# The expert gates G in HBM: by quarter of a tile, or by partition and block of eight expert tiles

## Chip, cores and metric

One Trainium2 chip, one core. The metric is the time of one execution on the device in microseconds; the kernel before takes 4118.97 us (median of 3 runs, 4109.92 to 4119.53).

## The reference

One step of a decoder layer: an input projection feeds a 4-head mLSTM and 8-head stick-breaking attention, their output is projected, gated and added, and then comes PEER, the part that matters here. Tokens: 1024 of a prompt and 64 of a sample, D = 1024.

```python
qry = (xf @ w_query).reshape(T, 8, 2, 128)
sa = einsum('thd,nd->thn', qry[:, :, 0], sub_keys_a)      # 128 scores
sb = einsum('thd,nd->thn', qry[:, :, 1], sub_keys_b)
va, ia = top_k(sa, 16); vb, ib = top_k(sb, 16)
top_s, pos = top_k(all 256 sums va + vb, 16)
experts = take(ia * 128 + ib, pos)                        # 16 per head, of 16384
gates = softmax(top_s)
act = gelu(einsum('tkd,td->tk', expert_u[experts], xf))
out = einsum('tk,tkd->td', gates * act, expert_v[experts])
```

## The kernel before

The phases follow one another: projection, gates, prompt_mix, sample_mlstm, sample_attention, and then the two that the change touches, `routing` (L1789) and `apply` (L2164), the expert stage.

**Two ways to the experts.** Of the nine token tiles of 128 rows, four (D0 to D1, 512 tokens, TD) are dense: for them all 16384 experts are computed and multiplied by a matrix of gates G that is zero but for the chosen ones. The other five (640 rows, the sample as a half tile of 64 picks) gather: for each of 576 picks, POOL fetches a row of expert_u and a row of expert_v per partition by indirect DMA.

**G** has one value for each expert (a, b), 128 by 128, and each dense token. The expert is numbered 128 a + b; b lies on the partitions. `routing` makes it: for each dense tile DVE builds one-hot matrices (`hot`, L2113), ACT scales one by the gates (`gate_a`, L2036), PE multiplies them for 8 tokens at a time (`spread`, L1976), and ACT copies the result from PSUM into G_stage, `gs`, [128, 3, 128 a, 32 t] (`keep` of ACT, L2042). G_stage has three buffers of a quarter tile (HT = 32 tokens) each. SP stores each quarter q (0 to 15) when its four copies are done (`keep` of SP, L1880, the DMA at L1883), in the queue in which it also loads w_query in pieces of 2 MB, two buffers (`load_query`, L1875), rows of x, and stores hf and the scores of gathered tiles. ACT writes quarter q only when the store of q - 3 has landed (L2045). The last lines of SP's program wait for all stores.

G_d is (16 quarters, 128 partitions, 128 a, 32 t) before: a store of a quarter is 16 KB in a row per partition on both sides.

**The expert stage** runs over a = 0 to 127 (an expert tile is one a: 128 experts, b on partitions) in 16 blocks of NBK = 8. For tile a: PE turns e_u (`turn`, L2341), ACT copies it to e_uT, PE makes the products with XT into psH (`products`, L2351; the turning of tile a + 1 stands inside the products of tile a), ACT applies Gelu into e_W, DVE multiplies by the gates (`weigh`, L2430), from e_g [128, 16 quarters, 8 a, 32 t], which holds one block in one buffer. In the first tile of a block, behind its products, PE sums the block before over its eight tiles with e_v in eight units (`sums`, L2361), and DVE adds each unit to Y (`add`, L2437).

**Picks** are worked off between: DVE does about 2.5 picks beside each tile and 2 beside each addition. One pick is a dot product of pick_u with the token rows (L2470) and, 12 picks later, a multiply-add of pick_v into acc (L2486). Five buffers for pick_u, four for pick_v; POOL issues the fetches (`fetch_u`, L2280; `fetch_v`, L2299) when DVE is done with a buffer. DVE also chooses the experts of the next gathered tile, in 29 pieces per tile, between the picks.

**SP's queue in the expert stage** (L2229): per tile it waits until the buffer of e_u (three of them) is turned and loads e_u; behind the e_u of tile 8b + 3 it waits until the eight tiles of the block before are weighed, and loads the gates of block b (`load_gates`, L2239, the DMA at L2243); behind the e_u of the tiles 8b + 4 to 8b + 7 two rows of e_v each. The gates of block 0 are issued between e_u of tile 0 and e_u of tile 1. The load of a block:

```python
sp.dma_start(g[:, :, :, :],
    G_d[:, :, b * NBK:(b + 1) * NBK, :].rearrange("q b a t -> b q a t")).then_inc(g_in, 16)
```

Per partition these are 16 runs of 8 x 32 floats, 1 KB.

Of the kernel before, what the change touches and what calls it, by code (L numbers as in the profile page):

```python
# [26 lines left out]
P = 128  # L27
# [18 lines left out]
PH, NK, DK, TK = 8, 128, 128, 16  # L46
NE = NK * NK
KX = PH * TK
HT = 32

D0, D1 = 4, 8
TD = (D1 - D0) * P
# [30 lines left out]
def build(nc, io):  # L83
    ctx = ExitStack()
    with ctx:
# [41 lines left out]
        def dram(name, shape, dt=F32):  # L127
            return nc.dram_tensor(name, shape, dt, kind="Internal").ap()
# [9 lines left out]
        with outer:  # L138
# [8 lines left out]
            with nc.sbuf_tensor("cols", [P, NT + 1, P], F32) as cols, \  # L147
# [12 lines left out]
                with nc.sbuf_tensor("hcat_s", [P, D], F32) as hcat_s, \  # L160
# [3 lines left out]
                                  past_k_in=[pool_dma_sem(f"past_k_in{n}") for n in range(4)])  # L164
                    phase(sample_mlstm, **shared)
                    phase(sample_attention, **shared)
        G_d = dram("G_d", (TD // HT, P, NK, HT))
        hf_d = dram("hf_d", (hf_at(NT) + NS, D))
        sc_d = dram("sc_d", (len(GATHER_TILES) - 1, P, 2 * PH, NK))
        with nc.sbuf_tensor("XT", [P, KD, TD], F32) as XT,              nc.sbuf_tensor("ids", [P, 2, KX], I32) as ids,              nc.sbuf_tensor("pick_gates", [P, 2, KX], F32) as pick_gates:  # L170
# [1618 lines left out]
def routing(nc, io, sem, mod_d, x1_d, XT, G_d, hf_d, sc_d, ids, pick_gates, **_):  # L1789
# [4 lines left out]
    NG, GT, NS_, NO = 4, 8, 3, 3  # L1794
# [8 lines left out]
    for j in range(ND):  # L1803
        n = len(rest)
# [14 lines left out]
    with ExitStack() as ctx:  # L1819
# [15 lines left out]
        oa, ob = sb("hot_a", [P, NO, GT, NK]), sb("hot_b", [P, NO, GT, NK])  # L1835
        gs = sb("G_stage", [P, NS_, NK, HT])
        psT, psQ, psS, psG = ps("r_psT", [P, D]), ps("r_psQ", [P, 512]), ps("r_psS", [P, 512]), ps("psG", [P, 2, GT, NK])
# [8 lines left out]
        g_stored = [sem(f"g_stored{i}") for i in range(NS_)]  # L1846
# [14 lines left out]
        def _(sp):  # L1861
# [18 lines left out]
            def keep(d, quarter):  # L1880
                q = d * (P // HT) + quarter
                sp.wait_ge(g_kept, d * (P // GT) + (quarter + 1) * HT // GT)
                sp.dma_start(G_d[q], gs[:, q % NS_, :, :]).then_inc(g_stored[q % NS_], 16)  # L1883

            load(0)
            for n, name in enumerate(("sub_keys_a", "sub_keys_b")):
# [4 lines left out]
            for j in range(-1, ND + 1):  # L1891
# [16 lines left out]
                if j >= 1:  # L1908
                    keep(j - 1, P // HT - 1)
            sp.wait_ge(hf_kept, 16 * len(GS))  # L1910
            sp.wait_ge(sg_kept, 16 * (len(GS) - 1))
            for i in range(NS_):
                sp.wait_ge(g_stored[i], 16 * len(range(i, ND * P // HT, NS_)))

# [249 lines left out]
def apply(nc, io, sem, pool_dma_sem, mod_d, x1_d, XT, G_d, hf_d, sc_d, ids, pick_gates, **_):  # L2164
# [3 lines left out]

    NBK, NU, NW, NY = 8, 3, 9, 4
    ND = D1 - D0
    NBLK = NK // NBK
    UNITS = 2 * ND
# [9 lines left out]
    with ExitStack() as ctx:  # L2184
# [7 lines left out]
        g = sb("e_g", [P, TD // HT, NBK, HT])  # L2192
# [11 lines left out]
        u_in, g_in, v_in = [sem(f"e_u_in{i}") for i in range(NU)], sem("e_g_in"), [sem(f"e_v_in{i}") for i in range(NBK)]  # L2204
# [25 lines left out]
        def _(sp):  # L2230
# [8 lines left out]
            def load_gates(b):  # L2239

                if b >= 1:
                    sp.wait_ge(weighed, NBK * b)
                sp.dma_start(g[:, :, :, :], G_d[:, :, b * NBK:(b + 1) * NBK, :].rearrange("q b a t -> b q a t")).then_inc(g_in, 16)  # L2243

            for a in range(NK):
                b, t = divmod(a, NBK)
# [330 lines left out]
```

## Time and profile before

| | |
|---|---|
| Runs | 4109.92, 4119.53, 4118.97 us; median 4118.97 |
| Profiled execution, span from the first to the last instruction | 4056.0 us (its own time isn't given beside it; the median is 63.0 us above the span) |
| Mean granted TensorE clock | 0.916 |
| Busy: PE, DVE, POOL, ACT | 86%, 68%, 38%, 22% of the span |
| Moved | 1044.35 MB, 257 GB/s over the span |
| Routing, expert stage | about 1337 to 1919 us, 1922 us to the end |
| Stores of G, loads of G | 16 and 16, 2 MB each, 12.0 and 26.1 us to landing (median) |

The profile is of one execution. Busy shares are averages over stages with different limits, so the stages are read one by one: by windows (busy time per engine, granted clock, share of 16 DMA engines, GB/s), by waits (which engine stood, for whom, how long in total, how many times, the longest), and by the DMA view of a window (packets and bytes of each queue; q0 is POOL's, q1 is SP's). A landing time is from the issue of a DMA to its completion. "Share" in a queue's row is the time that its packets took, of 16 engines over the window.

### The profile page before, as it was taken

How to read it: one execution, taken by the hardware profiler on the slowest of the kernel's cores; microseconds unless marked ns; L12 is line 12 of the kernel's file. 1: busy time of each engine (PE TensorE's matmuls, PEld its weight loads, DVE VectorE, ACT ScalarE, POOL GpSimd, SP SyncE). 2: the span in 40 equal slices, each digit the busy share in tenths (PEclk: the TensorE clock that was granted, in tenths of full speed). 3: DMA queues.
4: the chain of work that ended last, by engine and by line, in shares of the span. 5: the costliest groups of instructions: out<-in, count | busy, mean ns of one | idle time of the engine just before them, and what ended most of it. 6: DMA issues, size and time to landing. Idle time of an engine off the chain costs nothing.

```text
span 4056.0 us, 39947 instructions
## 1 busy us (share of the span) xinstructions
PE 3497.1 (86%) x13253; PEld 1966.8 (48%) x13253; DVE 2775.1 (68%) x5292; ACT 907.0 (22%) x1917; POOL 1556.6 (38%) x1400
## 2 busy tenths in 40 slices
PE   7999958888765688985899889899999898989995
PEld 3444435555552588885444444444444444444442
DVE  1222234566442378887698888988888988987787
ACT  0111115566321025546100111101110111101110
POOL 0000000000165000000565666666666666667675
PEclk9999966998877799998899999999999899999997
DMA  8222032110264456563998999999999999999997
GB/s 302 88 90 89 34 118 74 48 44 32 49 190 142 169 204 255 209 249 132 348 360 307 395 376 388 360 373 391 386 386 335 393 386 384 358 376 403 397 400 278
DMA packets 345757, 1044.35 MB, mean 257 GB/s; under 512 B 32160, under 2 KB 82640, under 8 KB 341392
## 3 DMA queue, kind: packets, MB, share of 16 engines
q0 software_dynamic: 184336, 667.00, 43.9%
q1 hardware_dynamic: 161216, 374.80, 25.4%
q8 instruction: 107, 1.75, 0.2%
q14 instruction: 98, 0.80, 0.1%
HBM read 974.27 MB, written 67.14 MB: 257 GB/s over the span
## 4 chain that ended last, share of the span: by engine, by line
DVE 20%; DMA 14%; POOL 8%; DVEq 5%; issue 4%; PE 1%; SPq 0%; ACT 0%; POOLq 0%
DMA pick_v<-in_expert_v,ids 13%; DVE acc L2486 10%; DVE e_junk L2470 6%; POOL pick_u L2296 4%; DVEq L2481 4%; POOL pick_v L2304 4%; PE psH L2356 1%; DVE e_away L1771 1%; DVE e_found L1774 1%; DVE e_W L2435 1%; DMA e_u<-in_expert_u 1%; DVEq L1737 0%; DVE e_spare L1732 0%; DVE e_ia L1731 0%; DVE e_va L1734 0%
## 5 line engine op out<-in xcount | busy, mean ns | idle before, releaser
L2356 PE MATMUL psH<-XT,e_uT 128*128 128x512 f32 x2048 | 966.0, 613 | 122.3 <-ACT e_uT L2393 122.3
L2369 PE MATMUL psY<-e_v,e_W 128*128 128x512 f32 x2048 | 891.0, 597 | 19.3 <-DVE e_W L2435 19.3
L2486 DVE SCALAR_TENSOR_TENSOR acc<-pick_v,pick_w,acc 128x1024 f32<-128x1024 f32 x571 | 733.5, 1285 | 231.8 <-DMA pick_v<-in_expert_v,ids 189.6
L2296 POOL DMA_INDIRECT pick_u<-in_expert_u,ids x576 | 712.1, 1236 | 393.6 <-DVE pick_dot L2470 259.0
L2304 POOL DMA_INDIRECT pick_v<-in_expert_v,ids x576 | 658.7, 1144 | 281.5 <-issue 161.3
L2470 DVE CUSTOM_DVE_ANT_0 e_junk<-pick_u,x_rows 128x1024 bf16<-128x1024 f32 x576 | 702.9, 1220 | 26.2 <-DMA pick_u<-in_expert_u,ids 14.0
L2369 PEld LDWEIGHTS psY<-e_v,e_W 128*128 128x128 f32 x2048 | 392.1, 192 | 515.6 <-issue 487.9
L2356 PEld LDWEIGHTS psH<-XT,e_uT 128*128 128x128 f32 x2048 | 380.2, 197 | 510.6 <-issue 369.7
L385 PE MATMUL ps_p<-w_in_sb,hT 128*128 128x512 f32 x1008 | 441.0, 597 | 0.0
L385 PEld LDWEIGHTS ps_p<-w_in_sb,hT 128*128 128x128 f32 x1008 | 190.9, 191 | 231.8 <-issue 231.7
L2393 ACT ACTIVATE e_uT<-psU 128x512 f32<-128x512 f32 x256 | 149.0, 594 | 638.0 <-PE psU L2348 637.9
L2397 ACT ACTIVATE pick_dot<-pick_dot 128x8 f32<-128x8 f32 x72 | 15.0, 208 | 1091.0 <-DVE pick_dot L2470 1091.0
L2269 POOL DMA_DIRECT2D e_scores<-sc_d x4 | 2.4, 589 | 585.5 <-POOLq L103 585.5
L2348 PEld LDWEIGHTS psU<-e_ident,e_u 128*128 128x128 f32 x1024 | 134.3, 147 | 174.4 <-issue 163.3
L1982 PE MATMUL psG<-hot_a,hot_b 128*128 128x128 f32 x1024 | 150.5, 309 | 77.3 <-ACT hot_a L2039 77.3
L1222 POOL MEMSET s_own<- 128x512 f32 x1 | 0.5, 524 | 520.3 <-POOLq L103 520.3
L2348 PE MATMUL psU<-e_ident,e_u 128*128 128x128 f32 x1024 | 160.9, 282 | 29.8 <-DMA e_u<-in_expert_u 29.8
L2039 ACT ACTIVATE hot_a<-hot_a,kT 128x128 f32<-128x128 f32 x512 | 156.2, 389 | 124.6 <-DVE hot_a L2118 124.2
L1982 PEld LDWEIGHTS psG<-hot_a,hot_b 128*128 128x128 f32 x1024 | 139.3, 219 | 86.5 <-ACT hot_a L2039 86.3
L1116 DVE TENSOR_SCALAR zb<-psZ,sb_bias_sb 128x128 f32<-128x128 f32 (+7 forms) x64 | 52.3, 817 | 151.9 <-PE psZ L903 150.3
L1953 PE MATMUL r_psQ<-hT_g,w_query_sb 128*128 128x128 f32 (+1 forms) x1280 | 147.3, 276 | 1.8 <-DVE hT_g L2106 1.0
L304 POOL DMA_DIRECT2D w_ada<-in_w_ada x16 | 14.5, 908 | 347.6 <-PE ps_m L356 267.8
(453 smaller groups left out, 3888.1 us busy)
## 6 DMA issues: line engine op xcount, KB each, us to landing
w_query_sb<-in_w_query SPq DMA_DIRECT2D x36, 2048.0 KB, 8.1
e_u<-in_expert_u SPq DMA_DIRECT2D x128, 512.0 KB, 7.2
e_v<-in_expert_v SPq DMA_DIRECT2D x128, 512.0 KB, 11.1
G_d<-G_stage SPq DMA_DIRECT2D x16, 2048.0 KB, 12.0
e_g<-G_d SPq DMA_DIRECT2D x16, 2048.0 KB, 26.1
w_ada<-in_w_ada POOLq DMA_DIRECT2D x16, 1024.0 KB, 10.1
w_in_sb<-in_w_in SPq DMA_DIRECT2D x7, 2048.0 KB, 19.3
pick_u<-in_expert_u,ids POOLq DMA_INDIRECT x576, 8.6
```

Source lines behind the costliest of these rows:

```text
L385: m = pe.matmul(ps_p[n % 4][:, :], hT[:, b, j, :], w_in_sb[:, j, c0:c0 + 512], start=j == 0, stop=j == KD - 1)
L1982: m = pe.matmul(psG[:, i % 2, t, :], ob[:, i % NO, t, :], oa[:, i % NO, t, :], start=True, stop=True)
L2039: m = act.activation(oa[:, i % NO, t, :], oa[:, i % NO, t, :], ACT.Copy, scale=kT[:, d % 2, 2, n * GT + t:n * GT + t + 1])
L2296: pool.indirect_dma_start(gu[:, i % NGU, :], None, io["expert_u"][0], bass.IndirectOffsetOnAxis(ids[:, q % 2, j:j + 1], 0)).then_inc(pu_in ...
L2304: pool.indirect_dma_start(gv[:, i % NGV, :], None, io["expert_v"][0], bass.IndirectOffsetOnAxis(ids[:, q % 2, j:j + 1], 0)).then_inc(pv_in ...
L2348: t = pe.transpose(psU[:, half, j * P:(j + 1) * P], u[:, a % NU, c * P:(c + 1) * P], ident[:, :])
L2356: m = pe.matmul(psH[a % 2][:, :], uT[:, a % 2, j, :], XT[:, j, :], start=j == 0, stop=j == KD - 1)
L2369: m = pe.matmul(psY[i % NY][:, :], W[:, (b * NBK + t) % NW, k * P:(k + 1) * P], v[:, t, half_cols(half)], start=t == 0, stop=t == NBK - 1)
L2393: act.activation(uT[:, a % 2, 4 * half:4 * half + 4, :], psU[:, half, :].rearrange("p (j e) -> p j e", e=P), ACT.Copy).then_inc(u_kept, 1)
L2470: dve.tensor_tensor_reduce(junk[:, :], gu[:, i % NGU, :], xg[:, :], 1.0, 0.0, ALU.mult, ALU.add, dot[:, i // PB % 2, i % PB:i % PB + 1]).t ...
L2481: dve.drain()
L2486: dve.scalar_tensor_tensor(out=sums_q, in0=gv[:, i % NGV, :], scalar=wgt[:, m % 2, o:o + 1], in1=sums_q, op0=ALU.mult, op1=ALU.add).then_i ...
```

## The change

G_d gets the partition as its outermost dimension, then the block of eight a, then the quarter. In HBM each partition has 16 blocks of 16 KB, 256 KB in all. The store of a quarter writes 16 runs of 1 KB per partition, 16 KB apart; the load of a block reads one run of 16 KB per partition. G_stage, e_g and their contents are as before, and so are all waits and the order of all instructions. NBK becomes a constant of the module.

```diff
@@ -47,6 +47,7 @@
 HT = 32
+NBK = 8
@@ -164,7 +165,7 @@
-        G_d = dram("G_d", (TD // HT, P, NK, HT))
+        G_d = dram("G_d", (P, NK // NBK, TD // HT, NBK, HT))
@@ -1880,7 +1881,7 @@ def keep(d, quarter)
-                sp.dma_start(G_d[q], gs[:, q % NS_, :, :]).then_inc(g_stored[q % NS_], 16)
+                sp.dma_start(G_d[:, :, q, :, :].rearrange("p m n t -> p m (n t)"), gs[:, q % NS_, :, :].rearrange("p (m n) t -> p m (n t)", n=NBK)).then_inc(g_stored[q % NS_], 16)
@@ -2168,7 +2169,7 @@ def apply
-    NBK, NU, NW, NY = 8, 3, 9, 4
+    NU, NW, NY = 3, 9, 4
@@ -2240,7 +2241,7 @@ def load_gates(b)
-                sp.dma_start(g[:, :, :, :], G_d[:, :, b * NBK:(b + 1) * NBK, :].rearrange("q b a t -> b q a t")).then_inc(g_in, 16)
+                sp.dma_start(g[:, :, :, :], G_d[:, b]).then_inc(g_in, 16)
```

## Rows read from the trace of the kernel before

**Rows 1.** The page: busy shares of the span; DMA share in tenths over 40 slices

```profile
PE 3497.1 (86%) x13253; PEld 1966.8 (48%) x13253; DVE 2775.1 (68%) x5292; ACT 907.0 (22%) x1917; POOL 1556.6 (38%) x1400
...
DMA  8222032110264456563998999999999999999997
```

**Rows 2.** Windows of routing and expert stage: us; busy us (instructions); PEclk, DMA share, GB/s

```profile
1600.00:1800.00 200.00, 170.72 (x1397) 167.24 (x1395) 170.06 (x524) 105.98 (x281) 0.00 (x0) 0.93 0.65 239
...
2500.00:3000.00 500.00, 463.93 (x1232) 215.68 (x1231) 438.76 (x766) 57.64 (x111) 335.20 (x284) 0.96 0.99 380
```

**Rows 3.** Waits of the expert stage, 1950 to 4056 us: total us, times, longest

```profile
DVE acc L2486 <- DMA pick_v<-in_expert_v,ids: 189.6, 115, 9.7
```

**Rows 4.** DMA issues by line over the span: KB each, median us to landing

```profile
w_query_sb<-in_w_query SPq DMA_DIRECT2D x36, 2048.0 KB, 8.1
...
e_v<-in_expert_v SPq DMA_DIRECT2D x128, 512.0 KB, 11.1
G_d<-G_stage SPq DMA_DIRECT2D x16, 2048.0 KB, 12.0
e_g<-G_d SPq DMA_DIRECT2D x16, 2048.0 KB, 26.1
...
pick_v<-in_expert_v,ids POOLq DMA_INDIRECT x576, 8.5
```

**Rows 5.** Windows behind the e_g issued at 2819.42 us

```profile
2819.42:2845.42 26.00, 26.00 (x62) 11.56 (x61) 24.61 (x45) 0.21 (x1) 19.12 (x16) 1.00 1.03 388
2845.42:2870.42 25.00, 25.00 (x59) 11.04 (x58) 22.97 (x44) 0.21 (x1) 19.01 (x16) 1.00 0.95 355
...
2885.42:2935.42 50.00, 41.01 (x121) 19.92 (x120) 41.27 (x90) 8.81 (x17) 31.28 (x27) 0.90 1.01 398
```

**Rows 6.** DVE's waits in five windows: from 3722.27, 3772.27, 2602.45, 2164.06 and 3077.58 us

```profile
DVE acc L2486 <- DMA pick_v<-in_expert_v,ids: 7.1, 7, 2.7
...
DVE acc L2486 <- DMA pick_v<-in_expert_v,ids: 16.4, 11, 2.7
...
DVE acc L2486 <- DMA pick_v<-in_expert_v,ids: 14.1, 5, 8.5
...
DVE acc L2486 <- DMA pick_v<-in_expert_v,ids: 8.4, 1, 8.4
...
DVE acc L2486 <- DMA pick_v<-in_expert_v,ids: 12.2, 5, 8.6
```

**Rows 7.** DMA queues, 2164 to 2184 us, behind the issue of the third e_g

```profile
q0 software_dynamic: 1158, 4.31, 60.0%
q1 hardware_dynamic: 2208, 2.62, 38.5%
```

**Rows 8.** DMA of 1912 to 1922 us: the last store of G alone

```profile
DMA packets 144, 2.10 MB, mean 210 GB/s; under 512 B 16, under 2 KB 16, under 8 KB 16
...
q1 hardware_dynamic: 144, 2.10, 49.6%
...
G_d<-G_stage SPq DMA_DIRECT2D x1, 2048.0 KB, 6.3
```

**Rows 9.** Instructions in order of time, 1905 to 1965 us: start, us

```profile
1923.82 0.53 SPq L2243 DMA_DIRECT2D e_g<-G_d  x1
...
1931.67 1.94 PE L2348 MATMUL psU<-e_ident,e_u 128*128 128x128 f32 x8 [20.18 <-DMA e_u<-in_expert_u]
...
1944.62 1.23 DVE L2470 CUSTOM_DVE_ANT_0 e_junk<-pick_u,x_rows 128x1024 bf16<-128x1024 f32 x1 [14.03 <-DMA pick_u<-in_expert_u,ids]
...
1947.67 1.12 PE L2348 MATMUL psU<-e_ident,e_u 128*128 128x128 f32 x4 [9.59 <-DMA e_u<-in_expert_u]
...
1957.45 0.69 DVE L2435 TENSOR_TENSOR e_W<-e_W,e_g 128x512 f32<-128x512 f32 x1 [8.48 <-ACT e_W L2414]
```

**Rows 10.** Window at the start of the expert stage

```profile
1936.00:1938.00 2.00, 2.00 (x3) 0.34 (x1) 0.00 (x0) 0.00 (x0) 1.60 (x2) 0.50 1.03 212
```

**Rows 11.** SP's issues in order of time; what PE waited for on w_query

```profile
1665.70 0.58 SPq L1883 DMA_DIRECT2D G_d<-G_stage  x1
...
1678.32 12.60 SPq L1878 DMA_DIRECT2D w_query_sb<-in_w_query  x2
...
  DMA w_query_sb<-in_w_query: 0.9, 1
```

## The prediction

> **What bounds the kernel now.** I read the page first: over the span PE is busy 86% and DVE 68%, but the DMA row of the 40 slices stands at 8 to 9 only from slice 20 on, which is the expert stage, from 1922 us to the end [rows 1]. By stage, the routing (1600 to 1800 us) uses its DMA engines 65% of the time at 239 GB/s, and the expert stage (2500 to 3000 us) 99% at 380 GB/s, with DVE busy 88% and PE 93% [rows 2]. So the question is which of DVE and DMA ends last, and where. The waits of the expert stage name it: DVE stood 189.6 us in all for rows of pick_v that had not landed, in 115 waits; there is no wait of DVE, PE or ACT for e_g at all [rows 3]. G's own transfers are 16 stores with a median of 12.0 us to landing and 16 loads with 26.1 us [rows 4].
>
> Inside a block of eight tiles (about 128 us) there are two phases. In the first, from the issue of e_g on, PE sums the block before and DVE does two picks beside each of eight additions. There DVE is the bound: 24.6 us busy of 26.0 and 23.0 of 25.0, while DMA moves 388 and then 355 GB/s [rows 5]. In the second, the tiles with their e_u and e_v, DMA runs at 398 GB/s and DVE falls to 41 us of 50 [rows 5]. The DVE waits agree: 7.1 us in the 50 us after one of the last e_g issues, 16.4 us in the 73 us behind it, and in an earlier block 14.1 us in the tile phase (8.5 of it one wait) [rows 6]. Looked at one block after the other, the 15 windows of 50 us behind the issues of the second to the last e_g hold 41 us of such waits; two of them are single waits of 8.4 and 8.6 us [rows 6] that stand near changes of the pick job, and leave 24 us that G's trickle can be charged with, 19 of it in the last three blocks. That 24 us is all the steady state can give back from the first phase.
>
> **The loads.** Each goes from 16 runs of 1 KB per partition to one of 16 KB. What a packet costs: in the 20 us behind the issue of the third load, queue 1 took 38.5% of 16 engines, 123 engine-us, for 2208 packets, and queue 0 60.0%, 192 engine-us, for 1158 packets, that is 0.166 us each [rows 7]. Queue 1's are about 2064 of the gates and 128 rows of e_u; these at 0.166 us are 21, and 102 are left: 0.050 us for 1 KB, 6.4 us of all engines per load. The price of 16 KB packets is in the last store, alone on the engines: 144 packets, 128 of them the data, 2.10 MB, 49.6% of 10 us x 16 = 79 engine-us, 0.62 us each, 5.0 us in all [rows 8]. That is written from SBUF, not read, but the nearest. So a load costs 1.4 us less of the engines; 16 loads 22 us. As the first phase is DVE's, this is hidden work but for the 24 us above.
>
> The Trainium skill ("DMA: Bandwidth & Descriptors", "Why small descriptors are slow (HBM only)") gives each packet some 3 extra cycles on 32-byte beats, 9% on 1 KB. By it a load would be 5.4 us against 5.0 and the saving 0.4 us; the rows give 28% and I go by them. The same page ("Latency and other measured facts") speaks against the change: with rows of 16 KB, large power-of-two pitches between partitions lower the rate, 207 GB/s at 512 KiB and 103 at 4 MiB against 214. The new pitch is 256 KiB, which it doesn't list; by 512 KiB a load would be 3% slower, 0.2 us. No run here shows it yet.
>
> **How the load shares the engines.** Today e_g gets 2.1 MB in some 24 us, 87 GB/s of 388, near one part in five, beside picks with packets of 4 KB: as if the queues took turns packet by packet. With 16 KB packets the turns give e_g four parts in five: 2.1 MB at about 320 GB/s, 6.5 us, and 8 us to landing instead of 26.1. In these 6.5 us the picks get about 80 GB/s; everything of theirs in flight comes about 5 us later, once per block. pick_v has four buffers; at a pick every 3.3 us, reissued 1 to 2 us after the buffer is spent, it is asked for some 11.5 us ahead and lands in 8.5 [rows 4]: 3 us of slack. 5 us late is then a stall of 2 us once per block, 30 us in 15 blocks. Against it stand the waits that the trickle causes now, 24 us, and relief afterwards (no e_g from 7 to 26 us behind the issue). Bounds from rows: the tile phase pushes 13 transfers of 0.5 MB past the picks and costs 5.6 us without its long wait, or 16.4 us in the last blocks [rows 6], 0.8 to 2.4 us per MB, thus 1.7 to 5.0 us per load of 2.1 MB, 26 to 75 us in 15; below, none at all, with 24 us gained. I take zero net: the added stall and the removed waits are of one size, and the first phase holds long DVE pieces of the choice between picks that refill the buffers. The e_u behind e_g in SP's queue (tile 8b+4) comes earlier too, but nobody waits for it.
>
> **The start of the stage.** Here the trickle is exposed. e_g(0) is issued at 1923.82, and e_u(1) behind it on the same queue. PE turns tile 0 at 1931.67 and then stands until 1947.67 for e_u(1), since the products of tile 0 hold the turning of tile 1 within them; ACT and DVE wait on these, and the first weighing is at 1957.45 [rows 9]. From 1936 to 1938 the engines moved only 212 GB/s at a share of 1.03 [rows 10]. Before e_u(1), queue 1 must move 0.75 MB of gate rows, 0.5 of e_u(0), 2.1 of e_g and 0.5: 3.9 MB. With 16 KB packets little of queue 0 slips in between, say 1.3 MB; 5.2 MB at 400 GB/s from 1924.5 is 1937.5, ten us earlier. The first dot (1944.62 [rows 9]) waits for everything together and gains only 3 to 4 us. Ends: 0 (DVE sets the pace from its first dot on) and -12. I take -8, since the weighing waits for PE's chain.
>
> **The stores.** They take over the 1 KB runs, 2048 of them instead of 128 packets. No row shows a write in 1 KB; nearest is the read in 1 KB, with the same pattern of strides: 6.4 us against 5.0. All but the last are covered: ACT waits for a store three quarters back, some 75 us. SP's w_query loads stand in the same queue behind them, but 12.6 us after the store (1665.70 and 1678.32), and PE waited 0.9 us in all for w_query [rows 11]. That cover holds as long as a store is done in some 12 us. The last store (6.3 us to landing [rows 8]) is waited for by the end of the phase: +1.4 us, taken as +1.5. Bounds: 0, and +4.5 with 2.1 MB at the 212 GB/s of [rows 10]. Instructions: one DMA each as before, nothing is added on SP, POOL or another queue, and no wait.
>
> **Sum.** -8 for the start, +1.5 for the last store, 0 for the steady state: -6.5 us on the span of 4056.0, 0.16%. The runs' median is 4118.97, 63 us above that span; these 63 us lie outside it and stay. Forecast: 4112 us, no difference that can be told: 0.3%, 12.4 us, is about what a measurement of this kernel can tell from none.
>
> **Rivals.**
> Contention shed (faster): the burst fits the slack of the pick buffers, and the waits of the first phase go. -8 + 1.5 - 24 = -30 us, 4089. For it: most blocks have no DMA wait at all behind e_g, so there is cover. Against: DVE-bound phases give back nothing more. Chance 0.34.
>
> Picks starve (slower): the 16 KB packets keep the picks from the engines 5 us at a time, pick_v has only 3 us of slack, and DVE, the bound of this phase, stands. It decides once a burst delays pick_v by more than about 3 us. Middle of the bounds: 3 us x 15 = 45, less 8, plus 1.5: +38, 4157; from 26 us it is +20. For it: DVE waits for pick_v whenever e_u and e_v load. The Trainium skill ("DMA: Bandwidth & Descriptors", "Queues, rings and completion order") has engines switch between queues by packet, which would make it so; e_g's share above agrees, one in five. Against: it is one short burst where the tile phase has four. Chance 0.16.
>
> Scattered stores (slower): all runs of one store lie 16 KB apart and partitions 256 KB apart. If that write goes at 105 GB/s, 20 us, the last store adds 14, and w_query loads come 7 us late some three times: +35, less 8, 4146. It decides at 12 us per store. For it: no write of the kind is in the trace; against: the reads with the same strides ran in a mix of 388 GB/s. Chance 0.09.
>
> That the change does not do what it says (the run of 16 KB is cut into smaller packets): then e_g gets a fair half at 4 KB and lands in 12 us. The stores of today, 16 KB on both sides, do travel as 16 KB packets [rows 8], so I give it little, and it ends within the forecast: start -5, 4115; it is in the forecast's share.
>
> **Numbers.** Forecast 0.41 with its own range of 4107 to 4131; faster 0.34; slower 0.16 + 0.09 = 0.25. The range for 8 in 10 runs from -41 us (12 us at the start, all 24 of waits, and some 5 of DMA capacity in the tile phase), 4078, to +34, 4153, most of the starving.
>
> **What the profile after would show.** e_g landing near 8 us, G_d above 6.3 at the last store; 128 data packets per load, 2048 per store; PE's wait for e_u(1) near 5 us instead of 16; DVE's waits for pick_v concentrated in the first 10 us behind each e_g issue, together near 190 us; stage from 1923 us to its end shorter by 8. Wrong if: DVE's total wait for pick_v moves by more than 15 us either way, if e_g still lands beyond 15 us, or if PE in the routing waits for w_query.

## The result and the profile after

The kernel after takes 4126.22 us (median of 14 runs, 4119.82 to 4136.56), the kernel before beside it 4112.61 us (14 runs, 4107.84 to 4119.53): ratio 1.0032, 95% interval 1.0023 to 1.0041. It is slower by 13.6 us, and the interval leaves no change out. The forecast was 4112, no difference, and its sign was not this one.

The profiled execution has a span of 4122.4 us, 66 us above the span shown of before, five times the difference of the medians. So the first thing to read is where the two spans part. The first lines are POOL's first instruction of the routing and the issues of the first and the last e_g, in order of time (start, us); this is the kernel after:

```profile
1391.56 0.23 POOL L1918 IOTA number_i<- 128x128 int32 x1 [37.20 <-POOLq L104]
...
1981.57 0.49 SPq L2244 DMA_DIRECT2D e_g<-G_d  x1
...
3909.37 0.33 SPq L2244 DMA_DIRECT2D e_g<-G_d  x1
```

and the same of the kernel before, in the execution that stands ahead of the prediction:

```profile
1336.00 0.23 POOL L1917 IOTA number_i<- 128x128 int32 x1 [36.71 <-POOLq L103]
...
1923.82 0.53 SPq L2243 DMA_DIRECT2D e_g<-G_d  x1
...
3844.90 0.38 SPq L2243 DMA_DIRECT2D e_g<-G_d  x1
```

55.6 of the 66 us lie ahead of the routing, in code that the change doesn't touch. From 1336.00 or 1391.56 on the change is read by stretches, each the difference of two such instants (the routing ends, for this table, with the issue of e_gate_s, at 1922.07 and 1979.80 us; before, again is a second profile of the kernel before, told of below):

| us | routing | e_g(0) to e_g(1) | e_g(1) to e_g(15) | e_g(15) to the end |
|---|---|---|---|---|
| before | 586.1 | 94.9 | 1826.2 | 211.1 |
| before, again | 584.8 | 94.4 | 1829.5 | 211.8 |
| after | 588.2 | 87.1 | 1840.7 | 213.0 |
| after less the mean of the two | +2.8 | -7.6 | +12.9 | +1.6 |

The sum is +9.7 us, near the 13.6 of the medians. Two stretches are as forecast, the third is not: the steady state loses 12.9 us in 14 blocks.

**The stores** cost what the sum had. The DMA view of ten microseconds (1969 to 1979 us) with the last store of the kernel after, beside [rows 8]:

```profile
DMA packets 2064, 2.10 MB, mean 210 GB/s; under 512 B 16, under 2 KB 2064, under 8 KB 2064
...
q1 hardware_dynamic: 2064, 2.10, 62.0%
...
G_d<-G_stage SPq DMA_DIRECT2D x1, 2048.0 KB, 7.7
```

62.0% of 10 us x 16 engines is 99 engine-us for 2064 packets, 0.048 us each, 6.2 us in all against 5.0 in one store of before; it lands 1.4 us later. PE's wait for w_query is 0.9 us in all, as in [rows 11].

**The loads** travel as forecast too. The queues in the 20 us behind the third e_g, beside [rows 7]:

```profile
q0 software_dynamic: 1223, 4.78, 64.1%
q1 hardware_dynamic: 288, 2.62, 30.9%
```

Queue 1 moves the same 2.62 MB in 288 packets in place of 2208, and takes 99 engine-us in place of 123.

**The start.** PE and DVE in order of time, beside [rows 9]:

```profile
1989.26 1.94 PE L2349 MATMUL psU<-e_ident,e_u 128*128 128x128 f32 x8 [21.46 <-DMA e_u<-in_expert_u]
...
1998.75 0.66 PE L2349 MATMUL psU<-e_ident,e_u 128*128 128x128 f32 x4 [3.08 <-DMA e_u<-in_expert_u]
...
2007.36 0.69 DVE L2436 TENSOR_TENSOR e_W<-e_W,e_g 128x512 f32<-128x512 f32 x1 [1.63 <-ACT e_W L2415]
```

From the issue of e_g(0) to the turning of tile 1 it is 17.2 us, 23.9 before; to the first weighing 25.8 us, 33.6 before. That is the gain of 7.8 us.

SP's queue shows one more difference, which the forecast didn't have. Before, the issue of e_u(1) behind e_g(0) takes SP 7.15 us:

```profile
1924.40 7.15 SPq L2249 DMA_DIRECT2D e_u<-in_expert_u  x1
```

and after, 0.72 us:

```profile
1982.10 0.72 SPq L2250 DMA_DIRECT2D e_u<-in_expert_u  x1
```

The issue behind each of the 16 loads takes 4.9 to 12.5 us before and 0.4 to 0.7 us after; behind loads in 4 KB packets (pad4k below) it takes 0.5 to 1.0 us. So e_u(1) was not only behind 2 MB of e_g(0) at the engines, its issue ended some 6 us later too. Which of the two counts for more isn't settled.

**The steady state.** The windows behind the e_g issued at 2873.04, the block of [rows 5] (the columns are the same):

```profile
2873.04:2899.04 26.00, 26.00 (x62) 11.55 (x61) 21.72 (x41) 0.21 (x1) 17.58 (x15) 1.00 1.01 400
2899.04:2924.04 25.00, 25.00 (x59) 11.02 (x58) 23.45 (x45) 0.21 (x1) 18.91 (x16) 1.00 0.91 320
...
2939.04:2989.04 50.00, 39.65 (x113) 18.95 (x112) 42.56 (x87) 9.31 (x18) 32.69 (x28) 0.90 1.02 401
```

In the first 26 us the engines move more than before, 400 GB/s and not 388, and yet DVE does less: 21.7 us of work and not 24.6. In the 25 us that follow, DMA is at 320 GB/s where it was at 355, and DVE gains only 0.5 us. The moment is seen in order of time, 10 to 14 us behind the issue:

```profile
2884.03 0.08 DVE L2471 DVE_READ_ACCUMULATOR2_ANT pick_dot<- 128x1 f32 x1
2886.76 1.28 DVE L2487 SCALAR_TENSOR_TENSOR acc<-pick_v,pick_w,acc 128x1024 f32<-128x1024 f32 x1 [2.64 <-DMA pick_v<-in_expert_v,ids]
```

A dot product ends, and the multiply-add behind it stands 2.64 us for its row of pick_v. That the whole loss of the steady state is such idle time is seen in the group of the multiply-adds from the second to the last e_g (count, busy, mean ns, idle before, and for whom). Before:

```profile
L2486 DVE SCALAR_TENSOR_TENSOR acc<-pick_v,pick_w,acc 128x1024 f32<-128x1024 f32 x500 | 642.3, 1285 | 201.5 <-DMA pick_v<-in_expert_v,ids 163.9 <-issue 0.4
```

and after:

```profile
L2487 DVE SCALAR_TENSOR_TENSOR acc<-pick_v,pick_w,acc 128x1024 f32<-128x1024 f32 x500 | 642.3, 1285 | 216.7 <-DMA pick_v<-in_expert_v,ids 162.1 <-issue 18.1
```

It is 201.5 us (206.5 in before, again) and 216.7 after, 10 to 15 us more, where the stretch is 11 to 15 us longer; DVE's busy time in it is the same within 0.5 us. Over 15 windows of each kind, from the second e_g on, DVE's idle time ahead of the multiply-add (some 0.3 us of each window is its ordinary gap) adds up to:

| us behind the issue of e_g | before | before, again | after |
|---|---|---|---|
| 0 to 10 | 7.6 | 8.9 | 4.4 |
| 10 to 20 | 13.9 | 16.1 | 44.2 |
| 20 to 30 | 12.5 | 14.0 | 5.9 |
| 30 to 50 | 28.2 | 27.9 | 25.6 |
| 50 to 110 | 137.4 | 134.7 | 129.7 |

The burst adds 28 to 30 us between 10 and 20 us and gives back 10 to 13 in the tens beside it, 2 to 3 from 30 to 50 us and 5 to 8 later. It isn't spread evenly: in the first four of the 15 windows the ten microseconds hold 0.3 to 1.4 us of idle time, in the next eight 2.4 to 3.5, in the last three 6 (2.3 to 5.5 there before). The total of DVE's waits that the profile puts down to pick_v is no help here: it is 189.2 us and was 189.6 [rows 3], since 18.3 us of the after's waits have no releaser named. The group's idle time counts them: 248.9 us, and 231.8 and 237.5 in the two profiles of before.

### The profile page after: what moved, and what is told of

Read it like the earlier page. It is cut to its first block, busy times and chain, and to the rows that moved or that the text cites. A ratio compares the mean times of both kernels' runs of the same rounds, so it can differ in the third digit from the quotient of the medians.

```text
span 4122.4 us, 39947 instructions
## 1 busy us (share of the span) xinstructions
PE 3512.6 (85%) x13253; PEld 1965.4 (48%) x13253; DVE 2775.0 (67%) x5292; ACT 906.3 (22%) x1917; POOL 1554.0 (38%) x1400
## 4 chain that ended last, share of the span: by engine, by line
DVE 20%; DMA 14%; POOL 8%; DVEq 5%; issue 4%; PE 1%; SPq 0%; ACT 0%; POOLq 0%
DMA pick_v<-in_expert_v,ids 14%; DVE acc L2487 9%; DVE e_junk L2471 6%; POOL pick_u L2297 4%; DVEq L2482 4%; POOL pick_v L2305 3%; PE psH L2357 1%; DVE e_away L1772 1%; DVE e_found L1775 1%; DVE e_W L2436 1%; DMA e_u<-in_expert_u 0%; DVEq L1738 0%; DVE e_spare L1733 0%; DVE e_ia L1732 0%; DVE Y L2444 0%
## 5 line engine op out<-in xcount | busy, mean ns | idle before, releaser
L2370 PE MATMUL psY<-e_v,e_W 128*128 128x512 f32 x2048 | 889.9, 596 | 16.9 <-DVE e_W L2436 12.5
L2487 DVE SCALAR_TENSOR_TENSOR acc<-pick_v,pick_w,acc 128x1024 f32<-128x1024 f32 x571 | 733.5, 1285 | 248.9 <-DMA pick_v<-in_expert_v,ids 189.2
L1983 PEld LDWEIGHTS psG<-hot_a,hot_b 128*128 128x128 f32 x1024 | 138.3, 217 | 88.2 <-ACT hot_a L2040 87.9
L1954 PEld LDWEIGHTS r_psQ<-hT_g,w_query_sb 128*128 128x128 f32 x1280 | 145.7, 193 | 2.2 <-issue 2.1
```

The costliest lines, as they stand in the source:

```text
L1954: m = pe.matmul(psQ[:, u * P:u * P + rows(k)], w_q[:, n % 2, j, u * P:(u + 1) * P], turned(k, j), start=j == 0, stop=j == KD - 1)
L1983: m = pe.matmul(psG[:, i % 2, t, :], ob[:, i % NO, t, :], oa[:, i % NO, t, :], start=True, stop=True)
L2370: m = pe.matmul(psY[i % NY][:, :], W[:, (b * NBK + t) % NW, k * P:(k + 1) * P], v[:, t, half_cols(half)], start=t == 0, stop=t == NBK - 1)
L2487: dve.scalar_tensor_tensor(out=sums_q, in0=gv[:, i % NGV, :], scalar=wgt[:, m % 2, o:o + 1], in1=sums_q, op0=ALU.mult, op1=ALU.add).then_i ...
```

## The experiments

Theory 1: packet size is what counts. A load in 16 KB packets holds the engines for some 6 us against the picks' 4 KB packets, and pick_v is asked for too short a time ahead. Theory 2: the place in HBM, partitions 256 KB apart, is what costs. Each kernel was timed in turn with the kernel before on one chip; the ratio is to those runs.

**1 KB packets in the new layout.** With padding behind each run the loads travel in 1 KB packets again. It also puts the partitions 320 KiB apart in place of 256.

```diff
-        G_d = dram("G_d", (P, NK // NBK, TD // HT, NBK, HT))
+        G_d = dram("G_d", (P, NK // NBK, TD // HT, NBK * HT + 64))
...
-                sp.dma_start(g[:, :, :, :], G_d[:, b]).then_inc(g_in, 16)
+                sp.dma_start(g[:, :, :, :].rearrange("p q a t -> p q (a t)"), G_d[:, b, :, 0:NBK * HT]).then_inc(g_in, 16)
```

> The layout after the change, but each run of 1 KB in HBM is followed by 256 bytes of padding, so that the load of a block again travels in 2048 packets of 1 KB; the store also writes 1 KB runs. Theory 1 (packet size: the 16 KB packets of a load keep the picks from the engines for some 6 us, pick_v has 3 us of slack, DVE stands about 2 us a block): the stalls 10 to 20 us behind each issue of e_g go back from 44 us in all to about 14, the gain of 8 us at the start of the stage goes too, the stores keep their cost: before + 2 us (ratio 1.000 to 1.001). Theory 2 (the place in HBM, partitions 256 KB apart, is what costs): still about 13 us slower than before (1.003).

Measured: 4116.14 us beside 4117.23, ratio 0.9999 (0.9990 to 1.0008). Idle 10 to 20 us behind the issues: 15.5 us. First interval 94.2, steady stretch 1826.8. The queues behind the third issue, against the two lines of after above:

```profile
q0 software_dynamic: 1208, 4.65, 61.6%
q1 hardware_dynamic: 2208, 2.62, 37.9%
```

Loss and gain are both gone, as theory 1 says. As the distance of the partitions has changed too, this run alone doesn't rule theory 2 out. Two others do: the next one has the loss with partitions 16 KiB apart, and the one with one burst (split, below) has loads of 1 KB packets at the unpadded 256 KiB and no loss.

**16 KB packets in the old layout.** The counterpart: loads of 16 KB from the layout of before. The 16 KB that lie together there are the gates of one quarter for all a, so this kernel multiplies by the wrong gates and its result is wrong; its transfers have the right sizes and number, and only the time is used.

```diff
-                sp.dma_start(g[:, :, :, :], G_d[:, :, b * NBK:(b + 1) * NBK, :].rearrange("q b a t -> b q a t")).then_inc(g_in, 16)
+                sp.dma_start(g[:, :, :, :].rearrange("p q a t -> p (q a t)"), G_d[b].rearrange("p a t -> p (a t)")).then_inc(g_in, 16)
```

> The layout of before with its stores in 16 KB; the load of a block takes the 16 KB per partition that lie together in HBM at index b of the first dimension, which are the gates of one quarter of a tile and not those of block b: the multiplication by the gates is done with wrong gates, all transfers have their sizes. Theory 1: the burst alone, with the gain at the start and without the cost of 1 KB stores: +15 for the bursts, -8 for the start, some 8 us slower than before (1.002), and stalls of about 44 us in all 10 to 20 us behind the issues. Theory 2: partitions lie 16 KB apart, so no slower than before, or 8 us faster.

Measured: 4125.41 us beside 4117.23, ratio 1.0026 (1.0017 to 1.0035). First interval 88.2, steady stretch 1844.6, idle in the ten microseconds 41.9 us. One of those windows (2884.84 to 2894.84 us), the groups of DVE (x count, busy, mean ns, idle before and for whom):

```profile
L2486 DVE SCALAR_TENSOR_TENSOR acc<-pick_v,pick_w,acc 128x1024 f32<-128x1024 f32 x2 | 2.6, 1284 | 2.7 <-DMA pick_v<-in_expert_v,ids 2.6
```

and the same window of the kernel before, 10 to 20 us behind its issue at 2819.42:

```profile
L2486 DVE SCALAR_TENSOR_TENSOR acc<-pick_v,pick_w,acc 128x1024 f32<-128x1024 f32 x3 | 3.8, 1283 | 0.3
```

Two multiply-adds in place of three. Large loads alone, with the old stores, make the loss, as far as the two intervals tell, and the gain at the start. The ratio was expected at 1.002.

**4 KB packets**, by padding behind every four runs (partitions 272 KiB apart).

> The layout after the change with 256 bytes of padding behind every four runs, so that a load of gates travels in packets of 4 KB, as large as those of the picks. Theory 1: e_g then gets about half of the engines for some 10 us; the stalls behind the issues lie between the 14 us of 1 KB packets and the 44 us of 16 KB, near 25; with some 6 us gained at the start and 2 lost on the stores 0 to 8 us slower than before (1.000 to 1.002). If packets above 1 KB all cost the same, as after: 1.003.

Measured: 4058.86 us beside 4054.45, ratio 1.0014 (1.0005 to 1.0022), as expected. The three sizes in one table, the first row from the kernel before, again, the last from after, its landing from the run with six buffers below, since its own profile has none:

| packet | e_g to landing, median | idle 10 to 20 us behind the issue | steady stretch | ratio |
|---|---|---|---|---|
| 1 KB | 26.3 us | 16.1 us | 1829.5 us | 0.9996 |
| 4 KB | 14.4 us | 29.3 us | 1837.6 us | 1.0014 |
| 16 KB | 10.9 us | 44.2 us | 1840.7 us | 1.0032 |

**The kernel before, again.**

> The kernel before once more, for a second profile of it. Its first profile had the front of the program, ahead of the routing, 55 us shorter than the profiles of all other kernels here. If that was one execution's, this one has the routing's first POOL instruction near 1391 to 1400 us and a span near 4115; the intervals between issues of e_g should agree with the first profile within 0.5 us in the mean, and the time with before.

Measured: 4050.77 us beside 4054.45, ratio 0.9996 (0.9986 to 1.0006), span 4049.0. The expectation on the front was wrong: POOL's first instruction of the routing is at 1326.75 us here. In this series, timed together on one chip, all kernels, the one before too, took 4048 to 4060 us and have fronts of 1327 to 1335 us; in three others, the result's among them, 4100 to 4126 us (after_v5 apart) and fronts of 1391 to 1401. So the short front is no matter of one execution or kernel. The record numbers the chips of the experiments: 9 and 12 have the short front, 5 and 7 the long one, and with it go some 60 us of the same code. What differs there isn't known. A span can be set against a median only where both are from the same series, which the 63 us of the prediction were not: here span and run differ by about 2 us.

**The lead of pick_v, first try:** five buffers for pick_v, four for pick_u, on the kernel after.

```diff
-    NGU, NGV, PB, LAG = 5, 4, 8, 12
+    NGU, NGV, PB, LAG = 4, 5, 8, 12
```

> The kernel after with five buffers for pick_v and four for pick_u (four and five before). Theory 1: pick_v is then asked for 3.3 us earlier, which covers a burst that makes it 5 us late with 3 us of slack; pick_u falls from 7 to 4 us of slack, near enough. The stalls 10 to 20 us behind e_g go from 44 us to under 20, the kernel is 15 to 30 us faster than after, so at or below the time of before. Theory 2: the time stays about 13 us above before, or grows by the buffer that pick_u has lost.

A miss: 4231.2 us beside 4117.23, ratio 1.0280 (1.0265 to 1.0295). POOL's waits in the stage, this run:

```profile
POOL pick_u L2297 <- DVE pick_dot L2471: 478.9, 216, 8.6
...
POOL pick_v L2305 <- DVE acc L2487: 8.4, 5, 3.7
```

and the kernel after:

```profile
POOL pick_u L2297 <- DVE pick_dot L2471: 251.7, 154, 7.0
...
POOL pick_v L2305 <- DVE acc L2487: 133.4, 74, 4.9
```

In this run POOL waits for pick_v's buffers nearly nowhere. POOL's program is fetch_u(i), then fetch_v(i - 13), in order. With five and four buffers fetch_u(i) waits for dot product i - 5, and fetch_v(i - 13) for multiply-add i - 17, which DVE does right behind dot product i - 5: two bounds on the same step, and either holds pick_v. A buffer moved from pick_u to pick_v tightens the first by one pick, for both rows, and loosens the second in vain. The lead of pick_v, from POOL's fetch of a row to the moment at which DVE is ready for it, is 8.0 us here and 10.8 in after (medians of picks 60 to 559), and the idle time 10 to 20 us behind the issues 76.4 us in place of 44.2.

**Six buffers for pick_u**, on both layouts (6, 4 in the same line).

> The kernel before with six buffers for pick_u in place of five. After the run with four and five buffers the theory reads: POOL issues the fetch of pick_v behind that of pick_u in one queue, and pick_u waits for its own buffer, so it is the number of pick_u buffers that sets how far ahead both are asked for; one more is 3.3 us more for both. Expected: DVE's idle time ahead of the multiply-adds falls by a good part of its 190 us, 20 to 80 us faster (0.98 to 0.995). If it is the engines' rate in the tile phase that holds the picks back and not the lead, no change.

> The kernel after with six buffers for pick_u. Theory 1 (the burst uses up the lead of the picks): with 3.3 us more lead the idle time 10 to 20 us behind each e_g falls from 44 us to under 15, and the kernel is no slower than the same with the layout of before: within 4 us of u6_before, or up to 8 us faster for the gain at the start. If the burst takes capacity that the picks need whatever their lead, it stays 13 us above u6_before.

Measured, in one series with before at 4054.45: 4048.22, ratio 0.9987 (0.9977 to 0.9997), and 4059.56, ratio 1.0014 (1.0004 to 1.0024). The gain that was expected from more lead, 20 us and more, didn't come, nor did the two layouts come together; the other branch of both expectations is nearer, no change before and 13 us between the two. DVE's waits of u6_before for pick_v are 189.5 us, as before; POOL's show why:

```profile
POOL pick_v L2304 <- DVE acc L2486: 348.3, 216, 4.9
...
POOL pick_u L2296 <- DVE pick_dot L2470: 26.4, 7, 11.4
```

POOL now stands for pick_v's four buffers and nearly never for pick_u's: pick_v's lead is held by the other bound and grows by 0.3 to 0.4 us only. In u6_after the idle time 10 to 20 us behind the issues is 42.8 us, nearly unchanged. Its steady stretch is 11.6 us shorter than after's, 1829.1, though; what that came from isn't settled, and the medians show 11 us between the layouts, as before. Six and five buffers together, which would loosen both bounds, were not tried.

**pick_v one pick earlier in POOL's program**, meant to move its lead without a buffer.

```diff
-            V_LAG = LAG + 1
+            V_LAG = LAG
```

fetch_v(i - 12) now stands behind fetch_u(i) and ahead of fetch_u(i + 1). With four buffers it waits for multiply-add i - 16, one step of DVE later than before, and DVE uses the row one step later too.

> The kernel after, POOL fetching the row of expert_v for a pick one pick earlier in its queue (12 behind the fetch of expert_u in place of 13), buffers unchanged. DVE uses a row of pick_v at the pick behind whose dot product it is spent, so this moves its fetch from three picks ahead to four, 3.3 us. Theory 1 (a burst makes pick_v some 5 us late on too short a lead): idle time 10 to 20 us behind the issues falls from 44 us to under 20, and the kernel is 10 to 25 us faster than after. If the lead is not what counts but the capacity that the burst takes, the time stays as after's, ratio 1.003 to before.

> The same one edit on the kernel before. DVE's idle time ahead of the multiply-adds is there 137 us in the tile phase, where the engines run at 392 to 410 GB/s. If the short lead causes it, 20 to 60 us faster than before (0.985 to 0.995); if the engines' rate does, within 5 us of before. Either way the difference between the two layouts should shrink from 13 us to under 5.

Measured, beside 4111.11: after with it 4106.99, ratio 0.9991 (0.9979 to 1.0002); before with it 4099.65, ratio 0.9974 (0.9961 to 0.9986). The edit takes 0.4% off the kernel after, by the ratios, and 0.26% off the one before. Of the expectations, 10 to 25 us faster than after came true (17 us by the ratios); 20 to 60 or under 5 us for before (11 measured), under 20 us of idle time behind the issues and under 5 us between the layouts did not. DVE's waits of vlag_before in the stage, against [rows 3]:

```profile
DVE acc L2486 <- DMA pick_v<-in_expert_v,ids: 89.5, 100, 1.4
DVE e_junk L2470 <- DMA pick_u<-in_expert_u,ids: 75.4, 64, 12.0
```

100 us less waiting for pick_v, but 75 for pick_u, which waited 14.0 us before, in one wait. And the lead of pick_v has hardly moved:

| | lead of pick_v | lead of pick_u | idle 10 to 20 us, multiply-adds | the same, dot products |
|---|---|---|---|---|
| before | 10.7 | 14.4 | 13.9 | 1.2 |
| after | 10.8 | 14.8 | 44.2 | 0.7 |
| u6_before | 11.0 | 15.0 | 14.2 | 1.2 |
| u6_after | 11.1 | 15.2 | 42.8 | 0.7 |
| vlag_before | 11.1 | 11.5 | 8.0 | 6.1 |
| vlag_after | 11.2 | 11.8 | 28.4 | 11.6 |
| vlag_u6_before | 11.1 | 11.5 | 9.7 | 4.4 |
| vlag_u6_after | 11.2 | 11.8 | 25.2 | 16.1 |

All in us; a lead is a median of picks 60 to 559, idle time a sum of 15 windows. What the edit really moves is pick_u, fetched 3 us later, behind pick_v. The 28.4 us of vlag_after look like a smaller burst, but with the 11.6 us that its dot products now stand they are 40.0, and between the layouts it is 26 us, against 28 to 30 without the edit.

Where the time came from is seen at a change of the pick job. In the kernel before POOL waits there until DVE has done the last dot product of the old job, fetches the first row of pick_u of the new one, and only then the next row of pick_v (3580.60 us), for which DVE has been ready since 3577.92:

```profile
3579.34 0.96 POOL L2296 DMA_INDIRECT pick_u<-in_expert_u,ids  x1 [0.30 <-issue]
3580.60 0.94 POOL L2304 DMA_INDIRECT pick_v<-in_expert_v,ids  x1 [0.30 <-issue]
...
3587.63 1.28 DVE L2486 SCALAR_TENSOR_TENSOR acc<-pick_v,pick_w,acc 128x1024 f32<-128x1024 f32 x1 [9.71 <-DMA pick_v<-in_expert_v,ids]
```

Four such waits, one per change, are 35.1 us, and 35.3 in the kernel after. In vlag_before that row is fetched at 3613.16, ahead of the wait, and only the first dot product of the new job stands:

```profile
3622.48 1.28 DVE L2486 SCALAR_TENSOR_TENSOR acc<-pick_v,pick_w,acc 128x1024 f32<-128x1024 f32 x1
3630.73 1.23 DVE L2470 CUSTOM_DVE_ANT_0 e_junk<-pick_u,x_rows 128x1024 bf16<-128x1024 f32 x1 [6.97 <-issue]
```

The four changes then cost 21.7 us in place of 35.1, and the idle time ahead of the picks' two instructions falls from 260 and 262 us in the two profiles of before to 234 in all. So about half of what was gained is POOL's order at the changes; what the other half came from isn't settled.

**The rest: lead or capacity?** The same with six buffers for pick_u, on both layouts.

> The kernel before with the fetch of pick_v one pick earlier and six buffers for pick_u. Alone, the earlier fetch gave 11 us, the sixth buffer 5 us, because POOL's queue then stood for pick_v's buffers. If both leads together count, 15 to 25 us faster than before (0.994 to 0.996) and less waiting of DVE for pick_u than the 75 us of vlag_before. If the engines' rate is the limit in the tile phase, as vlag_before.

> The kernel after with the same two edits. If all of the loss is lead, it is no slower than vlag_u6_before (within 3 us) and its steady stretch, from the second to the last issue of e_g, is as long within 3 us. If the burst takes capacity, it stays 7 us or more behind it.

Measured, beside 4052.89: 4036.77, ratio 0.9958 (0.9945 to 0.9971), and 4045.66, ratio 0.9986 (0.9978 to 0.9995). Steady stretches 1809.4 and 1821.8, 12 us apart, idle 9.7 and 25.2 us. The kernel before is 16 us faster with both edits, as expected, but DVE waits for pick_u 83.0 us, not less than the 75 of vlag_before. So the sixth buffer adds nothing in the steady stretch (vlag_before: 1809.0), and the burst costs as much as with five: 9 us by the medians (7 with five), 27 us in the ten microseconds. That is the branch that was expected if the burst takes capacity. What a burst takes is seen in ten microseconds behind an issue, here of u6_after (issue at 3069.51, 3069.5 to 3079.5 us):

```profile
q1 hardware_dynamic: 160, 2.18, 52.4%
q0 software_dynamic: 426, 1.55, 44.3%
...
pick_v<-in_expert_v,ids POOLq DMA_INDIRECT x3, 12.0
```

and of u6_before at its issue of the same block:

```profile
q0 software_dynamic: 673, 2.45, 70.0%
q1 hardware_dynamic: 863, 0.88, 28.7%
...
pick_v<-in_expert_v,ids POOLq DMA_INDIRECT x3, 9.5
```

The picks get 1.55 MB in place of 2.45, most of one pick (1.05 MB, 3.3 us of DVE's time) less, and land 2.5 us later (medians of three). The data fit a loss of capacity at a moment when DVE, the bound, can't do other work. But none of these runs gave pick_v more than 0.4 us of lead; the one that took some away (after_v5) has more idle time there, so whether one or two picks more of it would hide the burst stays open.

**The gain at the start, by order.** From the kernel before: `if a == 1` in place of `if a == 0` ahead of load_gates(0).

> The kernel before, with the gates of block 0 issued behind e_u of tile 1 in place of ahead of it. If the gain of 7.8 us at the start of the stage is e_u(1) no longer standing behind e_g(0) in SP's queue, this has all of it with nothing else changed: PE's wait for e_u(1) falls from 16 us to 8 or less, 6 to 9 us faster than before (0.998). If the gain had come from fewer or larger packets as such, no change.

Measured: 4114.61 us beside 4117.23, ratio 0.9990 (0.9979 to 1.0000), less than the 6 to 9 us expected and hardly told from none. The first interval is 90.2 us, 94.4 to 94.9 before: 4 to 5 us of the 7. PE no longer waits for e_u(1), as expected; but now the first weighing waits for the gates:

```profile
DVE e_W L2435 <- DMA e_g<-G_d: 3.5, 1, 3.5
```

**Smaller packets for e_v**, beside the late e_g(0): each e_v in two DMAs of half the columns, 2 KB.

> From the kernel before: the gates of block 0 behind e_u of tile 1, and each row block of expert_v in two DMAs of half its columns, so in packets of 2 KB in place of 4 KB. If queues share the engines by packet, smaller packets for e_v leave more to the picks in the tile phase, where DVE idles 137 us, while e_v is needed only at the end of the block: 10 to 30 us faster than before (0.993 to 0.998). Against it: each packet's own cost takes capacity there, and e_u stands behind e_v in the same queue and would come later, PE with it: then 5 to 20 us slower.

Measured: 4112.76 beside 4111.11, ratio 0.9998 (0.9984 to 1.0012). Steady stretch 1828.3, idle 50 to 110 us behind the issues 132.0: as before. At 2 KB against 4 KB nothing was gained or lost in the tile phase; both branches of the expectation failed, and why the smaller packets of e_v leave no more to the picks isn't known.

**One burst where it helps, none where it hurts.** The layout after; block 0 whole, the others as even and odd quarters, which leaves runs of 1 KB.

```diff
-                sp.dma_start(g[:, :, :, :], G_d[:, b]).then_inc(g_in, 16)
+                for par in range(2 if b else 1):
+                    qs = slice(par, None, 2) if b else slice(None)
+                    sp.dma_start(g[:, qs, :, :], G_d[:, b, qs]).then_inc(g_in, 16)
...
-                    dve.wait_ge(g_in, 16 * (a // NBK + 1))
+                    dve.wait_ge(g_in, 16 * (2 * (a // NBK) + 1))
```

> The layout after the change; block 0 is loaded in runs of 16 KB as there, the blocks from 1 on in two DMAs each, even and odd quarters, whose runs are 1 KB. Theory 1: the gain at the start (interval from e_g(0) to e_g(1) 88 us in place of 94) with the steady state of before: stalls of 14 us in all 10 to 20 us behind the issues, 3 to 6 us faster than before, less than a measurement can tell (0.998 to 1.000), and 17 us faster than after.

Measured: 4103.72 beside 4111.11, ratio 0.9976 (0.9964 to 0.9988): first interval 88.6, idle 10 to 20 us 15.3 us. Its loads of 1 KB packets have the partitions 256 KiB apart, as in after, so the loss isn't the place in HBM. It is 0.56% faster than after by the ratios, and a little better than expected: the steady stretch is 1820.5 us, 6 to 9 us shorter than before's, which two profiles of before can't settle as an effect.

**All together.**

> The layout after, block 0 in 16 KB runs, the other blocks in 1 KB runs by two DMAs, and the fetch of pick_v one pick earlier. If start, steady state and lead add up: 6 us at the start and 18 us in the steady state, with 0 to 2 us for the stores, 15 to 22 us faster than before (0.995 to 0.996). If the lead already hides the burst, no better than vlag_after (0.999).

> The same with six buffers for pick_u: 5 us more, 20 to 28 us faster than before (0.993 to 0.995), if both leads together count; else as split_vlag.

Measured, beside 4052.89: split with the earlier fetch 4032.27, ratio 0.9939 (0.9926 to 0.9952); with six buffers 4031.31, ratio 0.9947 (0.9934 to 0.9959). Both beat both kernels; they can't be told apart, so the sixth buffer isn't needed. The 21 us of the first are within the 15 to 22 expected; the 5 more of the second didn't show. By stretches split_vlag is 87.5 us in the first and 1807.5 in the steady one: the start of after and the steady state of vlag_before add up.

## Why the prediction was wrong

**The start** was right in its mechanism and its size: forecast -8, measured -7.6 in the first interval (-7.8 to the first weighing). e_u(1) came 6.7 us earlier, not ten, counted from the issue of e_g(0). The other 1.2 us lie between the turning of tile 1 and the weighing, 8.6 us in place of 9.8, at a granted clock of 0.80 in place of 0.70. PE's wait for e_u(1) is 3.1 us where it was 9.6: the prediction's "near 5 us instead of 16" counted the time from the turning of tile 0, in which PE also turned tile 0 and made products; by that count it is 9.5 us after, and the idle time alone is what [rows 9] show. late0 and big_both show the mechanism, e_u(1) standing behind e_g(0), from two sides. That its issue, too, took 7.15 us and now takes 0.72 was not in the prediction.

**The last store** was right: +1.5 forecast, +1.4 at its landing. Its packet price, taken over from reads of 1 KB (0.050 us), was 0.048 in the write. The whole routing is 2.8 us longer than in the mean of the two profiles of before; the routings of all kernels with 16 KB stores span 584.8 to 587.0 us and of those with 1 KB stores 586.3 to 588.7, so no more than 1 to 2 us can be read from them. Scattered stores as a rival did not happen: the last one took 6.2 us of the engines, far from 12. The Trainium skill ("DMA: Bandwidth & Descriptors", "Why small descriptors are slow (HBM only)") has some 3 extra cycles on a packet, by the prediction's estimate 9% on 1 KB. The last store shows 25%, 62.0% of the engines' time against 49.6%; the measurement decides.

**How the load shares the engines** was right in kind: the packets of 16 KB came, and the landing fell from 26.3 us to 10.9 (in u6_after). 8 was forecast; the picks kept 44% of the engines' time in the ten microseconds behind an issue of u6_after, where the forecast had a fifth for the load's 6.5 us. The Trainium skill's rule that engines switch between queues by packet ("DMA: Bandwidth & Descriptors", "Queues, rings and completion order") fits the three packet sizes in the table, in order if not in ratio. Its rule on large pitches (the same page, "Latency and other measured facts") starts at 512 KiB; here no run shows a loss at 256 KiB, as the kernel after, at 256 KiB, and big_both, at 16 KiB, have the same ratio within their intervals.

**The step that failed** is the netting of the steady state: "I take zero net: the added stall and the removed waits are of one size". The added stall was worked out as 2 us per block, 30 us in 15, and is 28 to 30 us. It stands 10 to 20 us behind the issues, not in the first 10, where the idle time fell, and not evenly, 6 us a block at the end and next to none at the start. The removed waits were taken as all 24 us that stood in the 50 us behind e_g. Only 10 to 13 us of them went in the tens beside the burst, 2 to 3 from 30 to 50 us, and 5 to 8 in the tile phase. A sum of 24 us was an upper bound ("all the steady state can give back"), and the prediction then used it as the expected value. Net +13 in the steady stretch in place of 0 is 13 of the 16 us by which the sum was off: -6.5 forecast, about +9.7 by the stretches, +13.6 by the medians. The stage from e_g(0) to the end is 5 to 9 us longer in place of 8 shorter. Of the prediction's own signs of being wrong none is clear: e_g lands within 15 us, PE doesn't wait for w_query, and DVE's total wait for pick_v is the same by name; only the idle time, with the waits of no named releaser, has moved, by 11 to 17 us.

The rival "picks starve", the one that happened, comes nearest at its lower end (26 us, less 6.5, is +20) and had 0.16 of the chance. It got so little because the fill from behind was believed. Its point of decision was 3 us of lateness; the one burst shown above has pick_v landing 2.5 us later, a median of three rows of u6_after, which neither confirms the 3 us nor speaks against them.

**The slack of pick_v** was about right: asked for 11.5 us ahead by the prediction, 10.7 in the median by the trace. Its origin was half of it: the four buffers of pick_v bind it (u6_before, vlag_before), but so do POOL's program order and pick_u's five on the same step (after_v5).

**The 63 us** between span and median were no part of the kernel: span and run of one execution differ by about 2 us, and the two came from different series, as the front shows.

## What to carry to other kernels

In this kernel a transfer that was hidden anyway gained nothing from larger packets, and beside a queue near its limit they took the engines from it in one piece: loads in 1 KB packets ran in the background, in 16 KB as a burst. So try large ones where somebody waits for the transfer or stands behind it in its queue, and small ones where only its competitors are waited for; e_v in 2 KB in place of 4 KB shows that it doesn't always pay. And where a term removes waits, what stands in the trace is its upper bound; it isn't the expected value until it is known which of them the term really ends.

## What was unexpected

Fetching pick_v one pick earlier in POOL's program, with no more memory, gave 0.26% without giving pick_v more lead, in part because an in-order program no longer held a needed fetch behind the change of a job. A fifth buffer of pick_v at pick_u's cost made it 2.8% slower, a sixth of pick_u alone 0.13% faster. The issue of a DMA behind a load in 2048 packets of 1 KB took SP up to 12.5 us, and behind one in 128 or 512 packets 1 us or less. The same front of the program took 1326 to 1338 us in some series and 1391 to 1401 in others, on other chips. And a pattern of 1 KB writes, 16 KB apart in each partition, ran at 0.048 us a packet, as fast as reads of that size.
